# Recurrence of a hybrid decoder step: score rows grouped by kind, products over 128 rows or columns, transposes for the turns

## The reference

```python
def step(S, inp):
    r_t, d_t, kk_t, a_t, k_t, v_t = inp
    sa = jnp.einsum('bhvk,bhk->bhv', S, -kk_t)
    S = S * d_t[:, :, None, :] + sa[..., None] * (kk_t * a_t)[:, :, None, :] + v_t[..., None] * k_t[:, :, None, :]
    return S, jnp.einsum('bhvk,bhk->bhv', S, r_t)
...
y = (y - mean) * lax.rsqrt(var + GN_EPS) * lnx_w + lnx_b
y = y + jnp.sum(r_h * k_h * r_k, axis=-1, keepdims=True) * v_h
y = y.reshape(B, T, D_RWKV) * g
```

## Time and profile before

| | |
|---|---|
| median of 3 runs | 2068.63 us (2068.09 to 2069.8) |
| span of the profiled execution, first to last instruction | 2065.7 us |
| median less span (start and end of an execution) | 2.9 us |
| TensorE busy | 1969.3 us, 95% of the span |
| VectorE, ScalarE, GpSimd busy | 1217.0, 615.1, 663.4 us |

### The profile page before, as it was taken

The page is one execution under the profiler, slowest core; times in us unless marked ns, Lnnn a source line. Parts: engine busy times, 40 slices in busy tenths (PEclk is TensorE's granted clock), DMA queues, the critical chain, the costliest instruction groups (busy, mean ns, idle before and its releaser), DMA issues.

```text
span 2065.7 us, 39742 instructions
## 1 busy us (share of the span) xinstructions
PE 1969.3 (95%) x15956; PEld 1237.7 (60%) x15956; DVE 1217.0 (59%) x2486; ACT 615.1 (30%) x1428; POOL 663.4 (32%) x774
## 2 busy tenths in 40 slices
PE   8999999988888998999988999999999999999999
PEld 6445656788886874455544545556656564747473
DVE  5375564366665548676655447856565655656473
ACT  5004543233433226666644222101010101101020
POOL 3000000244433002212203004556565656555561
PEclk9999999999999998999999999999999999999999
DMA  7000112200014811000036601111111111111112
GB/s 228 1 0 21 31 31 80 90 4 22 7 25 125 218 31 57 11 6 6 6 123 205 208 2 41 41 41 41 41 41 42 41 41 41 41 41 41 41 41 87
DMA packets 96661, 115.90 MB, mean 56 GB/s; under 512 B 32252, under 2 KB 68029, under 8 KB 96415
## 3 DMA queue, kind: packets, MB, share of 16 engines
q1 hardware_dynamic: 90718, 101.82, 15.8%
q10 hardware_dynamic: 3840, 6.29, 1.1%
q0 software_dynamic: 1920, 5.25, 0.8%
HBM read 104.75 MB, written 12.64 MB: 57 GB/s over the span
## 4 chain that ended last, share of the span: by engine, by line
PE 85%; DVE 9%; issue 3%; ACT 2%; DMA 1%; SPq 1%; POOL 0%; DVEq 0%; POOLq 0%; ACTq 0%
PE psum L1605 45%; PE psum L1608 33%; PE psum L2234 2%; PE psum L2116 2%; PE psum L2291 1%; DVE arena L2949 1%; DVE arena L3121 1%; DVE arena L3092 1%; DVE arena L2975 1%; ACT arena L1460 1%; DVE arena L3081 1%; SPq L874 0%; PE psum L1953 0%; DVE arena L3094 0%; DMA arena<-in_w_in_dram 0%
## 5 line engine op out<-in xcount | busy, mean ns | idle before, releaser
L1605 PE MATMUL psum<-arena 64*64 64x64 f32 (+16 forms) x11020 | 1025.0, 299 | 51.2 <-issue 21.1
L1605 PEld LDWEIGHTS psum<-arena 64*64 64x64 f32 (+6 forms) x11020 | 593.8, 143 | 386.4 <-issue 228.0
L1608 PE MATMUL psum<-arena 128*128 128x272 f32 (+1 forms) x2464 | 753.1, 467 | 6.3 <-DVE arena L3121 5.4
L1608 PEld LDWEIGHTS psum<-arena 128*128 128x128 f32 x2464 | 459.5, 190 | 298.9 <-issue 216.2
L3143 DVE TENSOR_TENSOR arena<-arena,psum 128x512 f32<-128x512 f32 x224 | 153.9, 687 | 217.1 <-PE psum L1608 216.2
L3121 DVE TENSOR_TENSOR arena<-arena,psum 128x272 f32<-128x272 f32 x328 | 141.6, 434 | 99.8 <-PE psum L1608 97.1
L1567 ACT ACTIVATE arena<-psum 128x272 f32<-128x272 f32 x64 | 25.4, 397 | 544.8 <-PE psum L1608 544.8
L1031 POOL TENSOR_TENSOR arena<-arena 128x512 f32<-128x512 f32 x17 | 21.6, 1271 | 360.9 <-DVE arena L2783 360.9
L1104 POOL TENSOR_TENSOR arena<-arena 128x544 f32<-128x544 f32 x49 | 65.8, 1343 | 165.0 <-PE psum L1608 165.0
L1460 ACT ACTIVATE arena<-psum,arena 128x640 f32<-128x640 f32 (+7 forms) x128 | 89.0, 699 | 52.1 <-DVE arena L2949 51.9
L1025 POOL TENSOR_TENSOR arena<-arena 128x256 f32<-128x256 f32 x82 | 61.5, 751 | 117.4 <-PE psum L1605 117.2
(11 more groups left out here) (327 smaller groups left out, 2015.1 us busy)
## 6 DMA issues: line engine op xcount, KB each, us to landing
arena<-in_w_up_dram SPq DMA_DIRECT2D x7, 2048.0 KB, 8.5
arena<-in_w_down_dram SPq DMA_DIRECT2D x7, 2048.0 KB, 7.8
arena<-in_cache_slc_kv_dram SPq DMA_DIRECT2D x96, 128.0 KB, 2.6
arena<-in_cache_cmp_kv_dram SPq DMA_DIRECT2D x72, 128.0 KB, 3.9
arena<-in_x_prompt_dram SPq DMA_DIRECT2D x16, 512.0 KB, 13.7
arena<-in_w_in_dram SPq DMA_DIRECT2D x13, 512.0 KB, 3.8
arena<-in_cache_cmp_kv_dram ACTq DMA_DIRECT2D x48, 128.0 KB, 3.7
arena<-in_w_in_dram SPq DMA_DIRECT2D x2, 2048.0 KB, 18.6
```

The source lines that it names most:

```text
L1605: return nc.tensor.matmul(out, lhsT, rhs, start=start, stop=stop)
L1608: return nc.tensor.matmul(out, lhsT, rhs, start=start, stop=stop, skip_group_check=True)
```

## The change

The score products now take both keys of a head at once: `kb` holds b and k of a chunk side by side (copied by ScalarE, `pair_act`), and one product of 64 rows, 128 weight columns and 128 moving columns puts the scores of k on partitions 0 to 63 and those of b on partitions 64 to 127. Values and `nu` stand in the same way (`nv_r`: values on the first half, `nu` on the second), and so do the key rows (`kt_rows`); the value and `nu` terms of state and outputs become one product over 128 rows. In `w_values` the second half of the scores is masked to zero, so that only the value term is added. Values and keys are turned by transposes of 128 rows. Since the scores of b no longer stand on both halves, the transpose of the matrix to be inverted is computed by eight more products (`a_product`) and copied by ScalarE (`at_act`). The bonus, gain and gate factors are folded by GpSimd (`gains_gated`), the square is taken by ScalarE (`square_act`), and some rings have two slots instead of three. The masked copies for the sample states are built by eight instructions on half the partitions instead of four on all.

```diff
@@ TensorE @@
-            def ar_product(c, hp):
-                for h in HALVES:
-                    ins = mm(shaped(banks[0][h, hp * P:(hp + 1) * P], 2, CH), ft[h, F_BK0 + hp, cols(c)], prs(h, hp, CH * c, CH))
-            def gk_product(c, hp):
...
-                for h in HALVES:
-                    ins = mm(shaped(banks[7][h, hp * P:(hp + 1) * P], 2, CH), ft[h, F_K + hp, cols(c)], prs(h, hp, CH * c, CH))
+            def score_product(c, i):
...
+                for hp in range(HP):
+                    ins = mm(shaped(banks[SCORE_BANK[i]][:, hp * P:(hp + 1) * P], 2, CH), kb[h, hp].rearrange("p a b -> p (a b)"), prs(h, hp, CH * c, CH))
-                for h in HALVES:
-                    ins = mm(banks[7][h, hp * CH:(hp + 1) * CH], ft[h, F_V + hp, cols(c)], ident[h, h])
+                for hp in range(HP):
+                    ins = nc.tensor.transpose(banks[5][HALVES[0], hp * P:(hp + 1) * P], ft[:, F_V + hp, cols(c)], ident)
-                for h in HALVES:
-                    for q, slot in enumerate((F_BK0, F_K)):
-                        ins = mm(banks[0][h, (q * HP + hp) * CH:(q * HP + hp + 1) * CH], ft[h, slot + hp, cols(c)], ident[h, h])
+                for hp in range(HP):
+                    ins = nc.tensor.transpose(banks[7][:, hp * P:(hp + 1) * P], kb[:, hp].rearrange("p a b -> p (a b)"), ident)
+            def a_product(c):
...
+                for hp in range(HP):
+                    for h in HALVES:
+                        ins = mm(banks[7][h, 256 + hp * CH:256 + (hp + 1) * CH], ft[h, F_BK0 + hp, cols(c)], ft[h, F_PR0 + hp, cols(c)])
+            def w_values(c):
...
+                    for i, (h, other) in enumerate(CROSSED):
+                        ins = mm_on(banks[6][other, hp * CH:(hp + 1) * CH], ag_r[c % 3][:, i, hp, 0, :], nv_r[c % 3][:, i, hp, :],
+                                    False, hp == HP - 1)
+            def state_product(c):
...
+                for hp in range(HP):
+                    for i, h in enumerate(HALVES):
+                        mm(banks[0][h, hp * CH:(hp + 1) * CH], kt_rows[c % 2][:, hp, i, :], nv_r[c % 3][:, i, hp, :])
-                    mm(out, tokbk[h, 0, hp, :], nu[h, hp, :], True, False)
-                    mm(out, tokbk[h, 1, hp, :], vtok[h, hp, :], False, True)
+            def y_values(c):
...
+                        ins = mm_on(banks[0][h, 256 + hp * CH:256 + (hp + 1) * CH], ag_r[c % 3][:, i, hp, 1, :], nv_r[c % 3][:, i, hp, :],
+                                    False, hp == HP - 1)
+            def sample_states():
+                pe.wait_ge(*once("rw_vb"))
+                pe.wait_ge(*once("rw_nub"))
...
+                    for i, h in enumerate(HALVES):
+                        mm(banks[q][h, :], kt_rows[NCH % 2][:, hp, i, :], nvb[i][:, hp, :, :].rearrange("p a b -> p (a b)"))
@@ ScalarE @@
+            def at_act(c):
...
+                nc.scalar.activation(at_r[c % 2], shaped(banks[7][:, 256:512], HP, CH), ACT.Copy).then_inc(sem("rw_toksb"), 1)
+            def pair_act(c):
...
+                for q, f in enumerate((F_K, F_BK0)):
+                    ins = nc.scalar.activation(kb[:, :, q, :], ft[:, f:f + HP, CH * c:CH * c + CH], ACT.Copy)
+            def square_act(c):
+                act.wait_ge(sem("rw_st_yc"), 2 * c + 2)
+                nc.scalar.activation(sqy, yc, ACT.Square).then_inc(sem("rw_yrs"), 1)
@@ VectorE @@
-                for hp in range(HP):
-                    rowm = spread(row_of, 2, HD)
-                    ins = tt(nub[:, hp], spread(nu[:, hp, :], 1, DEC_B), rowm, ALU.mult)
+                for h in range(2):
+                    for hp in range(HP):
+                        ins = tt(nvb[h][HALVES[1], hp], spread(nv_r[NCH % 3][HALVES[1], h, hp, :], 1, DEC_B),
+                                 spread(row_of[HALVES[1]], 2, HD), ALU.mult)
@@ GpSimd @@
+            def gains_gated(c):
+                bv, gtok = bv_r[c % 2], gtok_r[c % 2]
+                link(nc.gpsimd.tensor_tensor(bv, bv, lnb, ALU.add))
+                link(nc.gpsimd.tensor_tensor(bv, bv, gtok, ALU.mult))
+                nc.gpsimd.tensor_tensor(gtok, gtok, lnw, ALU.mult).then_inc(sem("rw_bv"), 1)
```

More of the change, by code:

```diff
@@ L216, in work, with ring @@
             return v
-        def ring(*dims):
-            return [work(*dims) for _ in range(3)]
+        def ring(n, *dims):
+            return [work(*dims) for _ in range(n)]
         at[0] = WR0
@@ L222, in decode_trunk @@
         amt = work(2, HP, CH)
-        wsb, nu, yc, bv = (work(HP, CH) for _ in range(4))
+        wsb, yc = (work(HP, CH) for _ in range(2))
         sqy = wsb
@@ new lines, in b_product, with keys_turned @@
+            def b_product(c):
+                if c >= 2:
+                    pe.wait_ge(sem("rw_wsb"), c - 1)
+                for hp in range(HP):
+                    for h, other in CROSSED:
+                        ins = mm(banks[6][other, 256 + hp * CH:256 + (hp + 1) * CH], ft[h, F_BK0 + hp, cols(c)], ft[h, F_PR0 + hp, cols(c)])
+                ins.then_inc(sem("rw_ab"), 1)
+            def keys_turned(c):
+                pe.wait_ge(sem("rw_toksb"), 3 * c + 2)
+                for hp in range(HP):
+                    ins = nc.tensor.transpose(banks[7][:, hp * P:(hp + 1) * P], kb[:, hp].rearrange("p a b -> p (a b)"), ident)
+                ins.then_inc(sem("rw_tok"), 1)
@@ L1891, in u_ready, with w_reads @@
-            def u_ready(c):
+            def w_reads(c):
+                for hp in range(HP):
+                    for h, other in CROSSED:
+                        out = banks[6][other, hp * CH:(hp + 1) * CH]
+                        if c < NCH:
+                            mm_on(out, ft[h, F_PR0 + hp, cols(c)], st[h, hp, :], hp == 0, False)
+                        else:
+                            mm_on(out, pst[h, hp, 0, :], ident[h, h], hp == 0, False)
+            def w_values(c):
+                pe.wait_ge(sem("rw_prod_sb"), 2 * c + 2)
+                pe.wait_ge(sem("rw_vgsb"), value_no(c))
+                for hp in range(HP):
+                    for i, (h, other) in enumerate(CROSSED):
+                        ins = mm_on(banks[6][other, hp * CH:(hp + 1) * CH], ag_r[c % 3][:, i, hp, 0, :], nv_r[c % 3][:, i, hp, :],
+                                    False, hp == HP - 1)
+                ins.then_inc(sem("rw_w_u"), 1)
@@ L2005, in _ @@
                     w_ready(n - 2)
-                for hp in range(HP):
-                    if outer:
-                        w_product(n - 2, hp)
-                    if new:
-                        value_turned(n, hp)
+                    w_reads(n - 2)
+                if new:
+                    value_turned(n)
+                if outer:
+                    w_values(n - 2)
                 if chain:
@@ L2030, in _ @@
                     tu_product(n - 1, 1, 1)
-                if outer:
-                    u_ready(n - 2)
-                for hp in range(HP):
-                    if new:
-                        b_product(n, hp)
-                        a_product(n, hp)
-                for hp in range(HP):
-                    if outer:
-                        u_product(n - 2, hp)
-                if n - 2 == NCH:
-                    sample_values()
+                if new:
+                    a_product(n)
                 if chain:
@@ L2045, in _ @@
                     x_product(n - 1, 2, 1)
-                if older and n - 3 < NCH:
-                    outputs_turned(n - 3)
+                if new:
+                    b_product(n)
+                if outer:
+                    u_product(n - 2)
+                if n - 1 == NCH:
+                    sample_reads()
                 if chain:
@@ L2050, in _ @@
                     tu_product(n - 1, 2, 1)
-                if n - 1 == NCH:
-                    sample_reads()
+                if older and n - 3 < NCH:
+                    outputs_turned(n - 3)
                 if n - 2 == NCH:
                     sample_states()
-                for hp in range(3):
-                    if prompt:
-                        state_product(n - 2, hp)
                 if chain:
@@ L2072, in _ @@
                 if outer:
-                    y_product(n - 2, 2)
-                    y_product(n - 2, 3)
+                    y_reads(n - 2)
+                    y_values(n - 2)
+                if new:
+                    keys_turned(n)
                 if n - 2 == NCH:
@@ L2080, in _ @@
                     x_product(n - 1, 4, 1)
-                for hp in range(HP):
-                    if new:
-                        gk_product(n, hp)
-                if chain:
                     tu_product(n - 1, 4, 0)
                     tu_product(n - 1, 4, 1)
-                for hp in range(1, HP):
-                    if new:
-                        keys_turned(n, hp)
                 if n - 2 == NCH:
```

381 lines of the change are left out of this document (190 added, 191 removed).

## The result

The changed kernel takes 2089.6 us (median of 4 runs, 2082.39 to 2092.7) against 2068.36 of the kernel before: a ratio of 1.0102, with an interval of 1.0083 to 1.0122. It is 1% slower; the forecast was 2064 us. The profiled execution is the fastest of its four, with a span of 2080.2 us.

What follows compares the result with a forecast made beforehand. TensorE was taken as the bound, partly starved of instructions: the period falls from 14.81 to 14.4 us, -6.6 us over 16 periods, and the end adds 2, so -4.6 gives 2064 us, range 2054 to 2084.

Steps and rivals of the forecast that it cites:

- first reading: TensorE bounds the recurrence; of its 14.81 us period, 2.2 us are not array work, mostly instruction supply.
- packets and matmuls: TensorE's list per period: about 402 matmuls instead of 468, and 3.30 instruction packets instead of 3.81.
- the price of a packet: Idle TensorE time per instruction packet: 0.58 us before, 0.12 taken after, 0.4 us a period.
- supply as the cause before: In the kernel before, most of TensorE's 2.2 us a period without array work is waiting for instructions.
- the price of the shape changes: TensorE's changes of tile shape: 13 a period at 0.10 us each, 1.3 us.
- rounds: Unit of TensorE work, 0.115 us: a float32 product with 64 columns on one quarter of the array.
- The open spot between the fifth `x_product` and its `tu_product`: The k scores no longer cover this place in TensorE's list; some 0.3 us stand open each period.
- 12.26 of work: TensorE's array work per period: 76 rounds 8.74 us, scores 1.76, gates 0.44, three fours of transposes 1.32.
- the head: Start of the recurrence: cleared rings and first key copy were to hide behind the last columns' transposes, costing nothing.
- The end: Sample states after the recurrence: eight masked copies 6.2 us, then products 3.5; +2 us against the kernel before.
- The first rival: TensorE's idle time is not supply or does not ease: 2093 us, or 2088 by packets; chance 0.2.
- The second rival: ScalarE's added copies hold the first `tu_product` by 0.25 us a period: 2068 us; chance 0.25, shared with half the stalls.

Runs made afterwards that it cites:

- experiment 7: Kernel before, with six of eight value turns of each chunk but the first left out; ratio 0.9966 to the kernel before.
- experiment 3: Changed kernel, with the second half of the score products right behind the first half; ratio 1.0088 to the kernel before.
- experiment 4: Changed kernel, with state reads, turned outputs and state products moved in TensorE's list to cover two open places; ratio 1.0093 to the kernel before.
- experiment 1: Changed kernel, with ScalarE's first key copies (chunk 0) ahead of its copies of the shifted rows; ratio 1.0078 to the kernel before.
- 11: Changed kernel, order rewritten and waits removed, plus earlier first-level mask, earlier value turn of chunk 1, later masking of second score half; ratio 0.9993 to the kernel before.
- experiment 5: Changed kernel, with 64 more already-satisfied waits a period on TensorE, 16 ahead of each pair of score products; ratio 1.0635 to the kernel before.
- experiment 6: Kernel before, with 64 more already-satisfied waits a period on TensorE, 16 ahead of each step of two score products; ratio 1.0381.

## Why the prediction was wrong

Its first reading was right as far as the result bears on it. "Issue" fell from 20.9 us to 0.5, packets and matmuls are as counted, and the price of a packet in the new list is nothing, where 0.12 us were taken. For supply as the cause before speak this, experiment 7, and one thing more in the trace of the kernel before. All 35 gaps of TensorE under "issue" in 387 to 628 us (over 0.15 us each, 21.2 us in all) end 2.25 to 2.96 us behind the start of an instruction packet, while the packets start 3.3 to 5.0 us apart; the packet of 451.14 us and the gap from 452.37 to 453.84 are one example. A period is 3.8 packets, so nothing that stands at a fixed place of the list could keep such a distance to them. No run took the packets away alone.

The step that failed in the period is the price of the shape changes. The Trainium skill, "TensorEngine Tiling (Array Packing)", Key Properties, states the drain and the forecast counted 13 of them, but at 0.10 us. TensorE's timeline of the changed kernel:

```profile
447.77 0.66 PE L1901 MATMUL psum<-ident,arena 128*128 128x128 f32 x4
448.36 1.87 PE L1676 MATMUL psum<-arena 64*64 64x64 f32 x48
450.03 0.66 PE L1679 MATMUL psum<-arena 64*64 64x64 f32 x16
450.62 0.63 PE L1853 MATMUL psum<-ident,arena 128*64 128x128 f32 x4
451.18 0.69 PE L1679 MATMUL psum<-arena 128*64 128x64 f32 x16
451.79 7.15 PE L1676 MATMUL psum<-arena 64*64 64x64 f32 x212
458.95 0.63 PE L2010 MATMUL psum<-ident,arena 128*64 128x128 f32 x4
459.70 2.02 PE L1676 MATMUL psum<-arena 64*64 64x64 f32 x64
```

The start of one row less that of the row above, set against the work of the row above: the key turn takes 0.59 to its successor where four transposes are 0.44; the state reads 0.59 where four rounds are 0.46; the value turn 0.56; the value terms 0.61 for 0.46. So 0.12 to 0.15 a change, and by experiment 3 0.19 around the scores. The first product behind a change is late, and the second is late again (0.10 us behind it where 0.05 is usual), which the forecast's 0.09 to 0.12 left out in part. The value turn and the value terms have the same tile, 128*64, in these rows, and yet the step from one to the other costs as much as the others: it is a fourteenth change, which the forecast did not count, and the trace does not say that a drain is what is paid. At 0.15 the 14 make 2.1 us, 0.8 more than the 1.3 of the forecast. The open spot between the fifth `x_product` and its `tu_product` was right: 448.36 to 450.03 is 1.67 us for 12 rounds of 0.115, 0.29 open against 0.3. Not forecast at all: `outputs_turned` to the fourth `x_product`, 0.75 us where four transposes and a change are 0.59, and the products behind it late again, some 0.3 in all, because VectorE's list holds them (experiment 4). 12.26 of work (8.74, 1.76, 0.44 and 1.32), 2.1, 0.29 and 0.3 are 14.95; measured 14.96. Without sample transposes the forecast was 14.25 (14.4 less 0.15): it had 0.8 too little for the changes, 0.3 too little for VectorE, and 0.4 too much for packets.

The second step that failed is the head, which "hides behind the transposes of the last columns". It does not: ScalarE's order puts `pair_act(0)` behind 2.2 us of other copies (experiment 1), and with that pause goes a lower granted clock, which with the copies early is 1.00 (experiment 1: 1.5 us of the first period). With the first three periods it is 4.9 and 6.7 us, more than half of the loss. Of the rest of the 6.7, the windows of the first two periods show that TensorE is longer at work: 8.32 and 12.52 us in experiment 1 (386.94 to 397.53 and 397.53 to 410.62), 6.98 and 10.19 in the kernel before (386.24 to 394.02 and 394.02 to 404.95). There the longer list has nothing to win back, since the first gap under "issue" of the kernel before comes at 409.9 us. That is 3.7 us; the forecast counted these periods as steady ones. The last 1.5 us, idle time of TensorE in the first period, stay open. The end was forecast at +2 us and is +4.1: the masked copies are as sized (6.10 us for 6.2), but the products behind them were priced at full clock, 3.5 us, and take 5.46 at the lower one.

The first rival named 2088 to 2093 us, and the time fell there, but by luck and by none of its mechanism: its idle time is gone. The second rival did not happen in the steady part: in 418 to 630 us the table of waits has none of TensorE for ScalarE, and the first `tu_product` starts right behind the value terms (451.79 us).

## What to carry to other kernels

Price a change that reorders an engine's list by its start and its end as well as by its steady period: here 16 us of 21 lie in the first three periods, the head and the end. A pause of TensorE can cost twice, once as the pause and once by the clock that is granted with it (experiments 1 and 11); at the end the clock was down already. Where TensorE is full, count each change of tile shape, and each step from transposes to products, as time, and gather products of one kind; and look which other in-order list carries work between two links of the chain.

## What the runs showed of the hardware

A wait on a semaphore that reached its value long before still costs TensorE 0.08 to 0.1 us of issue an instruction (experiment 5; in experiment 6 these instructions also follow one another at 0.1 us). A step from one kind of float32 products to another costs TensorE 0.12 to 0.15 us, also from transposes to products of the same tile, 128*64 (changed kernel, 450.62 to 451.79 us). In the kernel before, with 3.8 instruction packets in a period of 14.8 us, each gap of TensorE under "issue" over 0.15 us ended 2.25 to 2.96 us behind the start of a packet.
